# Turning the 64-slot expert's gated rows one step later, in a decoder trunk with a mixture of experts

## The chip, the cores and the metric

The kernel runs on one core of a Trainium2 chip. The metric is device time in microseconds (us) of one execution, lower is better. Five engines matter: TensorE (PE in the profile; its weight loads stand apart as PEld), VectorE (DVE), ScalarE (ACT), GpSimd (POOL) and SyncE (SP), which here only issues the loads of the weights. Each engine runs its own list of instructions in order; they wait for one another through semaphores, which only count up.

## The reference, cut to what matters

Two layers of a decoder run over 256 tokens of width 1024 in fp32. The last feed-forward layer is a mixture of experts: each token goes to 2 of 8 SwiGLU experts with a hidden width of 2816. The change touches only that layer.

```python
def swiglu(x, w1, w2):
    gate, up = jnp.split(x @ w1, 2, axis=-1)
    return (jax.nn.silu(gate) * up) @ w2

def moe_ffn(x, router_w, w1, w2):
    ...
    logits = (xt @ router_w).astype(jnp.float32)
    top_logit, top_idx = lax.top_k(logits, TOP_K)
    gates = jax.nn.softmax(top_logit, axis=-1)
    ...
    def expert_group(args):
        x_blk, e = args
        return swiglu(x_blk, w1[e], w2[e])

    yb = lax.map(expert_group, (xb, blk_expert)).reshape(cap, d)
    yb = yb * slot_gate[:, None].astype(yb.dtype)
    y = jnp.zeros_like(xt).at[slot_tok].add(yb)
```

## The kernel before

**Precision.** A product is made of three or so products of halves: ACT copies a chunk of weights of 128 x 2048 numbers (1 MB) into a rounded high part `whi` (L782, in `split_high`), and DVE subtracts it from the raw chunk, in place, which leaves the low part (L1883, in `split_low`; the trace calls its output `wlo`, `kvXr` or `raw6r` after the buffer). This is called a split here. Some chunks are not split (`WHOLE`): PE multiplies their raw fp32 numbers (L1660).

**Experts in pairs.** The eight experts are ordered by load and taken in four pairs. One of a pair has 128 token slots and is called full ("H"), the other has 64 and is called light ("L"). Each expert has 22 units of work: units 0 to 10 are the first product (two chunks each, giving 256 columns of gate and of up), units 11 to 21 the second product (one chunk each). An H chunk costs PE 12 matmuls (8 if it is not split), an L chunk 8: the light expert's 64 high and 64 low rows fill the 128 rows of the array together.

**Steps.** The function `turns()` gives the steps: step a has unit a % 22 of the full expert of pair a // 22, and the light expert's unit three steps behind (`LAG = 3`). So in steps 11, 12 and 13 of a pair the full expert is in its second product and the light one is still in its first. PE, ACT and DVE each go through the same list of steps with their own part of each, written out by hand. What the text calls step 11 is step 11 of a pair.

**A light unit.** After a light unit j of the first product ACT copies the low rows out of PSUM (L1125), DVE adds them to the high rows (L2478, `lsum`), ACT takes the silu (L1082), DVE multiplies gate by up (L2425, `light_gated`, into half j % 2 of `lgated`, which the trace shows as `arena`), PE transposes the product with two transposes (L1708, in `turn_light`), ACT makes the high copy (L1093, `light_hidden_hi`) and DVE the low copy (L2437, `light_hidden_lo`) in `xhL`. The second product of the light expert reads two rows of `xhL` in each unit (L1689 and L1690). The silu and `light_gated` of unit j stand in the next step, behind the splits which that step's full half asks for.

**Order in a step.** PE: full product; transposes of the full expert's previous unit (L1699); light product; `turn_light`; then, in some steps, spreading, selection or gathering for the next pair (L1585, steps 15 and 18). DVE: splits up to three ahead of the full half's last chunk; `light_gated`; full gating (L2461) and low copy (L2431); splits up to three ahead of the light half's last chunk; `lsum`; `light_hidden_lo`. ACT follows the same plan with its copies.

**Buffers and transfers.** `whi` has three slots (`HRING`): ACT may write the next high part once PE has used the chunk three splits back. Raw chunks have seven slots (`XRING`), and SP issues a load (L610) once PE has used the chunk seven back. A stream of one pair is 66 chunks, of which 58 are split.

Of the kernel before, what the change touches and what calls it, by code (L numbers as in the profile page):

```python
# [34 lines left out]
NF = DFF // P  # L35
# [118 lines left out]
def build(nc, x, mem, par, con, lvl, lin_w, ffn_w, out):  # L154
# [31 lines left out]
    with ExitStack() as ctx:  # L186
# [342 lines left out]
        def pair_no(p, i, j=0):  # L529
            return (p * PAIRS_E + i) * (NF // 2) + j + 1  # L530
# [171 lines left out]
        def _(act):  # L702
# [333 lines left out]
            def experts(p):  # L1036
# [63 lines left out]
                for a, (full, light) in enumerate(turns()):  # L1100
                    if full:
                        i, u = full
                        splits_through(SIDX["H", i, unit_chunks(u)[-1]])
                    if a == 1:
                        first_hi_of("L")
                    if behind:
                        light_silu(*behind)
                        behind = None
                    if full:
                        if u < NF // 2:  # L1110
                            act.wait_ge(w_used, unit_end(p, "H", i, u))
                            nc.scalar.activation(xsilu[:, u % 2, :], pb[:, u % 2, 0:S], ACT.Silu).then_inc(silu_ready, 1)
                        if 1 <= u <= NF // 2:
                            hidden_hi(i, u - 1)
                        if u == UNITS - 1:
                            act.wait_ge(selT_ready, nth(p, i))
                            act.wait_ge(w_used, unit_end(p, "H", i, u))
                            nc.scalar.activation(yHh.rearrange("p (a c) -> p a c", a=2), pb[:, 1:3, :], ACT.Copy,
                                                 scale=gs[:, 0:1]).then_inc(yH_hi, 1)
                    if light:  # L1120
                        i, u = light
                        splits_through(SIDX["L", i, unit_chunks(u)[-1]])
                        if u < NF // 2:
                            act.wait_ge(w_used, unit_end(p, "L", i, u))
                            nc.scalar.activation(low_rows[0:LIGHT, :], pb[LIGHT:P, 3 + u % 2, :], ACT.Copy).then_inc(low_ready, 1)  # L1125
                            behind = light
                        if 1 <= u <= NF // 2:
                            light_hidden_hi(i, u - 1)
                        if u == UNITS - 1 and i < PAIRS_E - 1:
                            act.wait_ge(w_used, unit_end(p, "L", i, u))  # L1130
                            nc.scalar.activation(yLh.rearrange("p (a c) -> p a c", a=2), pb[:, 4:6, :], ACT.Copy,
                                                 scale=gs[:, 1:2]).then_inc(yL_hi, 1)
                    if full:
                        i, u = full
                        if u == 9:
                            selections_turned(i)
                        if u in (15, 18) and i < PAIRS_E - 1:
                            gathered_hi(i + 1, (u - 15) // 3)
# [27 lines left out]
        def _(pe):  # L1166
# [387 lines left out]
            def experts(p):  # L1554
# [164 lines left out]
                for a, (full, light) in enumerate(turns()):  # L1719
                    if full:  # L1720
                        i, u = full
                        if u < NF // 2:
                            first_product("H", i, u)
                        else:
                            second_product("H", i, u - NF // 2).then_inc(w_used, 1)
                        if 1 <= u <= NF // 2:
                            turn_hidden(i, u - 1)
                    if a == 1:
                        gather_first("L")
                    if light and not full and light[1] == UNITS - 2:  # L1730
                        break
                    if light:
                        i, u = light
                        if u < NF // 2:
                            first_product("L", i, u)
                        else:
                            second_product("L", i, u - NF // 2).then_inc(w_used, 1)
                        if 1 <= u <= NF // 2:
                            turn_light(i, u - 1)
                    if full:  # L1740
                        i, u = full
                        if u in (5, 7) and i:
                            spread_outputs(i - 1, (u - 5) // 2)
                        if u == 9:
                            turn_selections(i)
                        if u in (15, 18) and i < PAIRS_E - 1:
                            gather(i + 1, (u - 15) // 3)
# [39 lines left out]
        def _(dve):  # L1787
# [612 lines left out]
            def experts(p):  # L2400
# [20 lines left out]

                def light_gated(i, j):

                    dve.wait_ge(lsilu_ready, pair_no(p, i, j))
                    V.tensor_tensor(lgated[0:LIGHT, j % 2, :], lsilu[0:LIGHT, :], lsum[0:LIGHT, S:2 * S],  # L2425
                                    ALU.mult).then_inc(lg_ready, 1)
# [22 lines left out]
                for a, (full, light) in enumerate(turns()):  # L2449
                    if full:  # L2450
                        i, u = full
                        splits_through(SIDX["H", i, unit_chunks(u)[-1]])
                    if a == 1:
                        first_lo_of(p, "L")
                    if behind:
                        light_gated(*behind)
                        behind = None
                    if full:
                        if u < NF // 2:
                            dve.wait_ge(silu_ready, full_no(p, i, u))  # L2460
                            V.tensor_tensor(xgated[:, u % 2, :], xsilu[:, u % 2, :], pb[:, u % 2, S:2 * S],  # L2461
                                            ALU.mult).then_inc(g_ready, 1)
                        if 1 <= u <= NF // 2:
                            hidden_lo(i, u - 1)
                        if u == UNITS - 1:
                            dve.wait_ge(yH_hi, nth(p, i))
                            V.scalar_tensor_tensor(out=yHl.rearrange("p (a c) -> p a c", a=2), in0=pb[:, 1:3, :],
                                                   scalar=gs[:, 0:1],
                                                   in1=yHh.rearrange("p (a c) -> p a c", a=2).bitcast(F32),
                                                   op0=ALU.mult, op1=ALU.subtract).then_inc(yH_lo, 1)  # L2470
                    if light:
                        i, u = light
                        splits_through(SIDX["L", i, unit_chunks(u)[-1]])
                        if u < NF // 2:
                            if u or i or p:
                                dve.wait_ge(lg_ready, pair_no(p, i, u) - 1)
                            dve.wait_ge(low_ready, pair_no(p, i, u))
                            V.tensor_tensor(lsum[0:LIGHT, :], low_rows[0:LIGHT, :], pb[0:LIGHT, 3 + u % 2, :],  # L2478
                                            ALU.add).then_inc(lsum_ready, 1)
                            behind = light  # L2480
                        if 1 <= u <= NF // 2:
                            light_hidden_lo(i, u - 1)
                        if u == UNITS - 1 and i < PAIRS_E - 1:
                            dve.wait_ge(yL_hi, p * (PAIRS_E - 1) + i + 1)
                            V.scalar_tensor_tensor(out=yLl.rearrange("p (a c) -> p a c", a=2), in0=pb[:, 4:6, :],
                                                   scalar=gs[:, 1:2],
                                                   in1=yLh.rearrange("p (a c) -> p a c", a=2).bitcast(F32),
                                                   op0=ALU.mult, op1=ALU.subtract).then_inc(yL_lo, 1)
                    if full:
                        i, u = full  # L2490
                        if u in (5, 7) and i:
                            add_outputs(i - 1, (u - 5) // 2)
                        if u == 10 and i < PAIRS_E - 1:
                            dve.wait_ge(selT_psum, nth(p, i))
                            select_pair(p, i + 1)
                        if u in (15, 18) and i < PAIRS_E - 1:
                            gathered_lo(i + 1, (u - 15) // 3)
# [113 lines left out]
```

## Time and profile before

| | us |
|---|---|
| median of three runs | 1476.75 (1472.2 to 1478.58) |
| the profiled execution, its own time | 1473.66 |
| its span, first instruction to last | 1471.6 |
| PE busy | 1406.7 (96% of the span) |
| DVE busy | 1100.4 (75%) |
| ACT busy | 904.4 (61%) |

The experts fill the last half of the span, from about 746 us on. A pair takes some 186 us: the wait of step 11 ends at 831.44 in the first pair and at 1018.04 in the second. In this document a time of a row is in us from the start of the span, and an idle time in square brackets is that of the engine just before the row, with what ended it.

### The profile page before, as it was taken

To read this page: it belongs to the slowest core of one execution; us is meant where nothing else is said; L and a number is where in the kernel's file an instruction comes from. 1 tells how busy PE (TensorE), PEld (TensorE's weight loads), DVE (VectorE), ACT (ScalarE), POOL (GpSimd) and SP (SyncE) were. 2 spreads that over 40 slices of the span, in tenths; PEclk is the share of its full clock that TensorE was granted. 3 is DMA by queue.
4 is the path that set the end of the run, shared out by engine and by line. 5 is a ranking of instruction groups with operands and counts; after the bars stand their busy time and mean duration, and the time that the engine had idled before them with its cause. 6 is when DMAs were issued, how large, how long until landed. Compare 5 with 4: busy or idle time off the path is not lost.

```text
span 1471.6 us, 19582 instructions
## 1 busy us (share of the span) xinstructions
PE 1406.7 (96%) x7795; PEld 1163.9 (79%) x7795; DVE 1100.4 (75%) x1188; ACT 904.4 (61%) x997; POOL 52.2 (4%) x58
## 2 busy tenths in 40 slices
PE   8999999999999999999999889998899988999986
PEld 7989898999989989898766676767767667767664
DVE  7878755645546878655778988888888898888986
ACT  6746444444436656444567866777767776777875
POOL 0031000000000031000000000000000000000000
PEclk9999999999999999999999999999999999999999
DMA  8443443445545343545499989999999998999993
GB/s 313 147 143 116 157 158 122 165 173 189 184 173 203 141 144 115 172 146 202 149 369 397 373 334 393 399 358 367 350 393 398 365 375 328 395 391 369 375 357 163
DMA packets 54482, 388.40 MB, mean 264 GB/s; under 512 B 6000, under 2 KB 6256, under 8 KB 8176
## 3 DMA queue, kind: packets, MB, share of 16 engines
q1 hardware_dynamic: 53840, 384.98, 69.1%
q10 hardware_dynamic: 544, 2.10, 0.4%
q8 instruction: 64, 1.05, 0.3%
q14 instruction: 34, 0.28, 0.1%
HBM read 386.00 MB, written 1.05 MB: 263 GB/s over the span
## 4 chain that ended last, share of the span: by engine, by line
issue 52%; PE 45%; DVE 2%; DMA 0%; ACT 0%; POOL 0%; POOLq 0%; DVEq 0%
PE pb L1201 13%; PE pb L1203 12%; PE pb L1202 12%; PE pb L1349 1%; PE pb L1431 1%; PE pb L1451 1%; PE pb L1182 1%; DVE xTl L1853 1%; DMA h<-in_x 0%; PE pb L1441 0%; PE pb L1408 0%; PE pb L1407 0%; PE pb L1300 0%; PE pb L1406 0%; DVE wlo L1804 0%
## 5 line engine op out<-in xcount | busy, mean ns | idle before, releaser
L1883 DVE TENSOR_TENSOR wlo<-raw,whi 128x2048 fp32r<-128x2048 f32 x134 | 303.8, 2285 | 70.3 <-ACT whi L782 69.8
L1804 DVE TENSOR_TENSOR wlo<-raw,whi 128x2048 fp32r<-128x2048 f32 (+1 forms) x101 | 226.0, 2247 | 132.7 <-ACT whi L714 132.3
L782 ACT ACTIVATE whi<-raw 128x2048 fp32r<-128x2048 f32 x134 | 254.6, 1914 | 101.1 <-PE pb L1203 63.8
L714 ACT ACTIVATE whi<-raw 128x2048 fp32r<-128x2048 f32 (+1 forms) x101 | 190.1, 1884 | 172.9 <-PE pb L1203 164.3
L1201 PE MATMUL pb<-xTh,whi 128*128 128x256 f32 x736 | 210.0, 285 | 2.0 <-DVE xTl L1841 1.2
L1202 PE MATMUL pb<-xTl,whi 128*128 128x256 f32 x736 | 208.2, 283 | 0.0
L1203 PE MATMUL pb<-xTh,wlo 128*128 128x256 f32 x736 | 208.2, 283 | 0.0
L1883 DVE TENSOR_TENSOR kvXr<-kvX,whi 128x2048 fp32r<-128x2048 f32 x65 | 147.8, 2285 | 29.8 <-ACT whi L782 29.5
L782 ACT ACTIVATE whi<-kvX 128x2048 fp32r<-128x2048 f32 x65 | 123.9, 1913 | 47.1 <-PE pb L1203 25.7
L1201 PEld LDWEIGHTS pb<-xTh,whi 128*128 128x128 f32 x736 | 141.1, 192 | 3.5 <-issue 1.9
L1657 PE MATMUL pb<-whi,xg 128*128 128x512 f32 x352 | 141.2, 401 | 1.1 <-DVE wlo L1883 0.7
L1202 PEld LDWEIGHTS pb<-xTl,whi 128*128 128x128 f32 x736 | 141.2, 192 | 0.1
L1203 PEld LDWEIGHTS pb<-xTh,wlo 128*128 128x128 f32 x736 | 141.1, 192 | 0.0
L1201 PE MATMUL pb<-whi,xg 128*128 128x512 f32 x224 | 90.8, 406 | 1.0 <-DVE wlo L1883 0.6
L1203 PE MATMUL pb<-whi,xg 128*128 128x512 f32 x224 | 88.0, 393 | 0.0
L1201 PE MATMUL pb<-whi,xTh 128*128 128x512 f32 (+1 forms) x224 | 86.1, 385 | 0.7 <-DVE xTl L1853 0.6
L1203 PE MATMUL pb<-whi,xTl 128*128 128x512 f32 (+1 forms) x224 | 84.4, 377 | 0.0
L1202 PE MATMUL pb<-wlo,xTh 128*128 128x512 f32 (+1 forms) x224 | 84.3, 376 | 0.0
L1883 DVE TENSOR_TENSOR raw6r<-arena,whi 128x2048 fp32r<-128x2048 f32 x33 | 75.3, 2283 | 10.6 <-ACT whi L782 10.3
L1657 PEld LDWEIGHTS pb<-whi,xg 128*128 128x128 f32 x352 | 66.2, 188 | 16.4 <-issue 2.3
L1658 PE MATMUL pb<-wlo,xg 128*128 128x512 f32 x200 | 78.3, 391 | 0.0
L1201 PE MATMUL pb<-whi,xhTh 128*128 128x512 f32 x176 | 75.2, 428 | 1.1
(410 smaller groups left out, 2823.1 us busy)
## 6 DMA issues: line engine op xcount, KB each, us to landing
raw<-in_ffn_w SPq DMA_DIRECT2D x184, 1024.0 KB, 7.1
kvX<-in_ffn_w SPq DMA_DIRECT2D x76, 1024.0 KB, 7.3
raw<-in_lin_w SPq DMA_DIRECT2D x64, 1024.0 KB, 4.9
arena<-in_ffn_w SPq DMA_DIRECT2D x37, 1024.0 KB, 7.3
raw<-in_lin_w SPq DMA_DIRECT2D x4, 536.0 KB, 5.4
arena<-in_mem ACTq DMA_DIRECT2D x2, 1024.0 KB, 7.9
h<-in_x SPq DMA_DIRECT2D x1, 1024.0 KB, 5.1
out<-xn SPq DMA_DIRECT2D x2, 512.0 KB, 3.1
```

The lines of the kernel that those rows point to most:

```text
L714: nc.scalar.activation(whi[:, m % HRING, c], raw[:, m % RING, c], ACT.Copy).then_inc(hi_ready, 1)
L782: nc.scalar.activation(whi[:, split_no(p, n) % HRING, :], xraw_slots[slot], ACT.Copy).then_inc(hi_ready, 1)
L1182: mm = nc.tensor.transpose(pb[:, turn_bank(no, b), i * S + t * P:i * S + (t + 1) * P], xn[:, t, k * P:(k + 1) * P], ident)
L1201: nc.tensor.matmul(o, lh, rh, start=first, stop=False)
L1202: nc.tensor.matmul(o, lh, rl, start=False, stop=False)
L1203: return nc.tensor.matmul(o, ll, rh, start=False, stop=last)
L1349: mm = nc.tensor.matmul(pb[:, b + hd % 2, i * P:(i + 1) * P], K[r, o + t * P:o + (t + 1) * P], Q[r, o + t * P:o + (t + 1) * P], start=True ...
L1431: mm = nc.tensor.matmul(pb[:, 4 + hd, t * S:(t + 1) * S], qX[:, 2 * hd + k, t * P:(t + 1) * P], kX[:, 2 * hd + k, :], start=(k == 0), stop ...
L1657: nc.tensor.matmul(o, both, w[0][:, kk, :], start=first, stop=False)
L1658: mm = nc.tensor.matmul(o, both, w[1][:, kk, :], start=False, stop=last)
L1804: V.tensor_tensor(wlo[:, m % RING, c], raw[:, m % RING, c], whi[:, m % HRING, c].bitcast(F32), ALU.subtract).then_inc(lo_ready, 1)
L1883: V.tensor_tensor(xlo_slots[slot], xraw_slots[slot], whi[:, split_no(p, n) % HRING, :].bitcast(F32), ALU.subtract).then_inc(lo_ready, 1)
```

## The change

`turn_light`, `light_hidden_hi` and `light_hidden_lo` of unit j run in the step of light unit j + 2 instead of j + 1, on PE, ACT and DVE alike. Since the transposes of unit j - 2 may now still be to come when `light_gated` wants to write unit j into the same half of `lgated`, DVE gets a wait for them.

```diff
@@ ACT
-                        if 1 <= u <= NF // 2:
-                            light_hidden_hi(i, u - 1)
+                        if 2 <= u <= NF // 2 + 1:
+                            light_hidden_hi(i, u - 2)
@@ PE
-                        if 1 <= u <= NF // 2:
-                            turn_light(i, u - 1)
+                        if 2 <= u <= NF // 2 + 1:
+                            turn_light(i, u - 2)
@@ DVE
                 def light_gated(i, j):
 
+                    if p or i or j >= 2:
+                        dve.wait_ge(lhid_turned, pair_no(p, i, j) - 2)
                     dve.wait_ge(lsilu_ready, pair_no(p, i, j))
...
-                        if 1 <= u <= NF // 2:
-                            light_hidden_lo(i, u - 1)
+                        if 2 <= u <= NF // 2 + 1:
+                            light_hidden_lo(i, u - 2)
```

In the middle of a pair the engines' lists read the same as before, since each step still has one pair of transposes; they belong to the unit before. The lists differ at the two ends. PE, the first step that had transposes of the light expert (step 4, `-`) and the first that has them now and had none (step 15, `+`, ahead of the gathering for the next pair):

```order
@@ -4128,5 +4128,4 @@
 L1657 MATMUL pb<-whi,xg 128x512
 L1658 MATMUL pb<-raw6r,xg 128x512
-L1708 MATMUL pb<-consts,arena 128x64 x2
 L1201 MATMUL pb<-whi,xg 128x512
 L1202 MATMUL pb<-kvXr,xg 128x512
@@ -4468,4 +4467,5 @@
 L1689 MATMUL pb<-whi,xhL 128x512
 L1690 MATMUL pb<-kvXr,xhL 128x512
+L1708 MATMUL pb<-consts,arena 128x64 x2
 L1585 MATMUL pb<-sel,xnh 128x192
 L1585 MATMUL pb<-sel,xnl 128x192
```

The last pair of transposes of a light expert moved from the end of step 14, where the light product of unit 11 ends, to the end of step 15. ACT, the same two places; its high copy in step 15 stands between the splits and the copies of the gathered rows (L1068):

```order
@@ -425,5 +425,4 @@
 L782 ACTIVATE whi<-raw 128x2048 [waits w_used,x_loaded3]
 L1125 ACTIVATE arena<-pb 64x512 [waits w_used]
-L1093 ACTIVATE xhL<-pb 128x2x64 [waits lhid_turned]
 L782 ACTIVATE whi<-raw 128x2048 [waits w_used,x_loaded4]
 L1082 ACTIVATE arena<-arena 64x256 [waits lsum_ready]
@@ -503,4 +502,5 @@
 L782 ACTIVATE whi<-raw 128x2048 [waits w_used,x_loaded3]
 L782 ACTIVATE whi<-raw 128x2048 [waits w_used,x_loaded4]
+L1093 ACTIVATE xhL<-pb 128x2x64 [waits lhid_turned]
 L1068 ACTIVATE xg<-pb,params 128x192 [waits gathered]
 L1068 ACTIVATE xg<-pb,params 128x192
```

One high copy left the list at step 4 and one came in at step 15. DVE in the middle of a pair, before:

```order
L1883 TENSOR_TENSOR kvXr<-kvX,whi 128x2048 [waits hi_ready]
L2425 TENSOR_TENSOR arena<-arena 64x256 [waits lsilu_ready]
L2461 TENSOR_TENSOR xgated<-xsilu,pb 128x256 [waits silu_ready]
L2431 TENSOR_TENSOR xhTl<-pb,xhTh 128x256 [waits hT_hi]
L1883 TENSOR_TENSOR wlo<-raw,whi 128x2048 [waits hi_ready] x2
```

and DVE at the same place in the changed kernel, whose lines from L2424 on are numbered two higher:

```order
L1883 TENSOR_TENSOR kvXr<-kvX,whi 128x2048 [waits hi_ready]
L2427 TENSOR_TENSOR arena<-arena 64x256 [waits lsilu_ready,lhid_turned]
L2463 TENSOR_TENSOR xgated<-xsilu,pb 128x256 [waits silu_ready]
L2433 TENSOR_TENSOR xhTl<-pb,xhTh 128x256 [waits hT_hi]
L1883 TENSOR_TENSOR wlo<-raw,whi 128x2048 [waits hi_ready] x2
```

The gated product kept its place behind the splits and has one wait more. SP's list is the same in both.

## Rows read from the trace of the kernel before

**Rows 1.** Waits, 760 to 1471 us: who waited <- for whom: total, times, longest.

```profile
PE pb L1708 <- DVE arena L2425: 34.2, 24, 2.9
...
PE pb L1657 <- DVE wlo L1883: 0.7, 2, 0.4
```

**Rows 2.** Windows: PE, PEld, DVE, ACT, POOL busy (count), granted clock, DMA share, GB/s.

```profile
748.00:1453.00 705.00, 666.49 (x2755) 490.20 (x2753) 603.40 (x515) 516.18 (x487) 0.00 (x0) 0.99 0.95 370
...
817.40:857.70 40.30, 32.39 (x139) 24.88 (x138) 39.46 (x36) 32.12 (x31) 0.00 (x0) 0.96 0.98 375
```

**Rows 3.** Timeline, PE, first pair, steps 7 and 10 to 16: start, duration, instruction, idle.

```profile
789.05 0.34 PE L1708 MATMUL pb<-consts,arena 64*128 64x64 f32 x2 [0.83 <-DVE arena L2425]
...
822.25 0.34 PE L1708 MATMUL pb<-consts,arena 64*128 64x64 f32 x2 [0.83 <-DVE arena L2425]
822.52 0.50 PE L1201 MATMUL pb<-whi,xhTh 128*128 128x512 f32 x1
...
831.44 0.34 PE L1708 MATMUL pb<-consts,arena 64*128 64x64 f32 x2 [1.99 <-DVE arena L2425]
...
839.51 0.33 PE L1708 MATMUL pb<-consts,arena 64*128 64x64 f32 x2 [1.10 <-DVE arena L2425]
...
847.52 0.33 PE L1708 MATMUL pb<-consts,arena 64*128 64x64 f32 x2 [1.10 <-DVE arena L2425]
...
855.53 0.47 PE L1708 MATMUL pb<-consts,arena 64*128 64x64 f32 x2 [2.89 <-DVE arena L2425]
855.94 0.79 PE L1201 MATMUL pb<-whi,xhTh 128*128 128x512 f32 x1
...
861.22 0.54 PE L1689 MATMUL pb<-whi,xhL 128*128 128x512 f32 x1
...
863.20 0.25 PE L1585 MATMUL pb<-sel,xnh 128*128 128x192 f32 x1
...
864.97 0.41 PE L1201 MATMUL pb<-whi,xhTh 128*128 128x512 f32 x1
...
867.72 0.39 PE L1689 MATMUL pb<-whi,xhL 128*128 128x512 f32 x1
```

**Rows 4.** Timeline, DVE, first pair, steps 10 to 15.

```profile
819.58 2.29 DVE L1883 TENSOR_TENSOR wlo<-raw,whi 128x2048 fp32r<-128x2048 f32 x1 [0.46 <-ACT whi L782]
...
828.77 2.28 DVE L1883 TENSOR_TENSOR raw6r<-arena,whi 128x2048 fp32r<-128x2048 f32 x1
...
836.84 2.27 DVE L1883 TENSOR_TENSOR wlo<-raw,whi 128x2048 fp32r<-128x2048 f32 x1
839.04 0.41 DVE L2425 TENSOR_TENSOR arena<-arena 64x256 f32<-64x256 f32 x1
...
844.85 2.29 DVE L1883 TENSOR_TENSOR wlo<-raw,whi 128x2048 fp32r<-128x2048 f32 x1 [0.19 <-ACT whi L782]
...
852.86 2.29 DVE L1883 TENSOR_TENSOR kvXr<-kvX,whi 128x2048 fp32r<-128x2048 f32 x1 [0.19 <-ACT whi L782]
...
863.47 4.49 DVE L1883 TENSOR_TENSOR wlo<-raw,whi 128x2048 fp32r<-128x2048 f32 x2 [5.59 <-ACT whi L782]
```

**Rows 5.** Windows around the stretches at half clock, columns as in Rows 2.

```profile
854.00:862.00 8.00, 6.47 (x17) 5.10 (x18) 3.88 (x4) 1.68 (x3) 0.00 (x0) 0.57 0.60 254
1018.00:1023.00 5.00, 4.96 (x16) 3.94 (x17) 5.00 (x4) 1.66 (x3) 0.00 (x0) 0.66 0.91 383
1226.00:1234.00 8.00, 6.38 (x17) 5.02 (x18) 3.97 (x4) 1.68 (x3) 0.00 (x0) 0.57 0.63 253
1414.00:1419.00 5.00, 5.00 (x16) 3.95 (x16) 1.93 (x2) 0.68 (x2) 0.00 (x0) 0.66 0.63 264
```

**Rows 6.** Windows of 20 us, DMA in the last two columns.

```profile
850.00:870.00 20.00, 17.11 (x73) 13.82 (x72) 14.06 (x18) 11.39 (x12) 0.00 (x0) 0.83 0.76 297
...
890.00:910.00 20.00, 19.88 (x75) 13.41 (x74) 15.47 (x9) 12.47 (x9) 0.00 (x0) 1.00 1.01 421
```

**Rows 7.** Timeline, PE, the wait of step 14 in the second pair.

```profile
1043.65 0.27 PE L1708 MATMUL pb<-consts,arena 64*128 64x64 f32 x1 [2.91 <-DVE arena L2425]
```

## The prediction

> **What bounds the kernel now.** I read the waits first, then the windows, then the timelines of PE and DVE side by side. The waits say that PE, in the whole stretch of the experts, waits for one thing: 34.2 us in 24 places before L1708, the transposes of the light expert, for DVE's gated product L2425; the next cause, a split, is 0.7 us [rows 1]. The window over the experts has PE busy 666.5 of 705 us [rows 2], so most of its idle time is this wait. The timeline shows where: in each pair six times, in step 7 (0.83 us) and in steps 10 to 14 (0.83, 1.99, 1.10, 1.10, 2.89; 7.91 us together) [rows 3]. The other three pairs repeat it.
>
> Why is the gated product late? DVE runs it behind the splits of its step: the split from 836.84 to 839.11, then L2425 at 839.04, then PE goes on at 839.51 [rows 3, 4]. And DVE is full there: busy 39.5 of 40.3 us in 817.4 to 857.7 [rows 2]. So from step 10 to 14 DVE, not PE, sets the pace, and the decisive question is not how much PE waits at L1708 but for what it would wait in its place: the low part of the chunk of its next product, which the same DVE makes just ahead of the gated product.
>
> The last wait is of another kind. At 852.64 PE has done step 14's products, and the splits of step 15 are done or due soon, but it stands until 855.53 for a product whose transposes nobody needs soon. Because PE uses nothing meanwhile, whi's three slots stay full, ACT can't copy, and DVE then idles 5.59 us before 863.47 [rows 4]. PE also runs at half its clock after it: granted clock 0.57 over 854 to 862 and over 1226 to 1234, and 0.66 over 1018 to 1023 and 1414 to 1419 [rows 5], which is 6.9, 6.9, 3.4 and 3.4 us at the level of 1.2 GHz.
>
> **The change part by part.** *The wait at L1708.* With the transposes of unit j - 2 instead of j - 1, the gated product that they need was made a whole step earlier, 7 to 10 us before. The 34.2 us go as waits of L1708. I follow the first pair to see what takes their place. Work of PE in a step is the distance of two L1708 rows less the idle time of the second: 7.20, 6.97, 6.91 and 5.12 us for steps 11 to 14, of which the transposes are 0.27 (822.25 to 822.52) [rows 3].
> - Step 10 ends for PE at 821.42. Transposes, 821.69. The split of step 11's first chunk ends at 821.87 [rows 4]; PE starts at 821.9 (before 822.52).
> - Step 11: 6.93 more, 828.8, transposes 829.1; but the next chunk's split ends at 831.05 [rows 4]. DVE has no gap before it, so nothing that PE does earlier brings it forward. Start 831.1 (before 831.7).
> - Step 12: 6.70, 837.8, transposes 838.1; split ends 839.11. Start 839.15 (before 839.8).
> - Step 13: 6.64, 845.8, 846.1; split ends 847.14, of which DVE's gap of 0.19 goes, since ACT gets its slot earlier. Start 847.0 (before 847.8).
> - Step 14: 4.85, 851.85, transposes 852.1, with no wait. Step 15: the full product takes 2.75 (864.97 to 867.72), 854.9; the light chunk's split, 855.15 before, is 0.4 earlier without the two gaps of 0.19, so just in time; 1.9 for the light product (861.22 to 863.20 was 1.98, a little of it at half clock); transposes 0.27; gathering 1.77 (863.20 to 864.97): step 16 starts at 858.8.
>
> Before, step 16 started at 864.97 [rows 3]. So the pair gains 6.15 us: of 7.91 us of waits some 4.5 us stay, as waits for splits, 3.45 go, and 2.7 are the clock: the full product of step 15 took 5.28 (855.94 to 861.22) instead of 2.75, the transposes 0.41 instead of 0.27. In step 7, PE would go on at 788.22 + 0.27, and only the split just ahead of the gated product holds it, 0.33 us before L2425 ends; there 0.6 of 0.83 goes. For the waits alone: 4 x (3.45 + 0.6) = 16.2 us.
>
> *The clock.* The half-clock stretches cost 2.7 us where PE came out of the long wait into one of 6.9 us (twice), and 1.7 us, half of 3.4, where all of it was work (twice): 8.8 us [rows 3, 5]. Three of the four are next to a wait of 2.9 us, the one at 1018 to a wait of 1.96; but the wait of 2.91 at 1043.65 [rows 7] has none. The longest wait that I expect to stay is some 2 us (829.1 to 831.1). So the two long stretches should go, and I count one of the short ones as staying: 8.8 - 1.7 = 7.1 us.
>
> *DVE's new wait* (44 times). Behind it queue the splits. It asks for transposes of unit j - 2, which PE issues right after light product j, while the same L2425 already needs that product, ACT's copy, `lsum` and the silu. It is met when DVE comes there. The row with two waits, if it cost anything, would leave gaps, and DVE has 0.8 us of idle time in 40 us [rows 2]. I take nothing; from the other side, that idle time spent again in each pair would be 3 us.
>
> *The copies one step later on ACT and DVE.* The same number of instructions. In step 15 one copy comes in on each; DVE has 5.59 us of idle time after it [rows 4]. Who needs the result? The second product reads unit c's rows in step c + 14, the copies of unit 0 now come in step 5, those of unit 10 in step 15 for step 24. Nothing. The transfers: SP's list is unchanged, its loads start when PE lets a slot go, so earlier.
>
> *What is late next.* After step 15 DVE and PE both run 6 us earlier, and DVE's gap of 5.59 us is gone. The transfers had pauses there (share 0.76, 297 GB/s) [rows 6]. A pair moves 66 chunks, 69.2 MB; in 186.6 - 6.75 = 180 us that is 385 GB/s against 371 now. The window 890 to 910 shows 421 GB/s at a share of 1.01 [rows 6], so they should keep up, with less in hand.
> The Trainium skill speaks against it: "DMA: Bandwidth & Descriptors", Specifications, gives about 358 GB/s as what HBM yields to one core. By that rule a pair could not be under 69.2 / 0.358 = 193 us, the transfers would already be the bound and the change would bring nothing. The trace disagrees: 370 GB/s over 705 us, 421 in a window.
>
> **Sum.** 16.2 + 7.1 = 23.3 us off the profiled execution's own 1473.66: 1450.4. The three runs lie 1.5 us below to 4.9 above that execution, their median 3.1 above; the median less the same sum is 1453.5. I take 1452, about midway, which is to count from 1475.3; the rivals below count from there too.
>
> **The rivals.**
> - *The clock stays.* Waits of some 2, 1 and 1 us for splits remain in steps 11 to 13, and the fall at 1018 came after such a one. Then only the 16.2 us go: 1459.
> - *DVE takes back nearly all.* Each wait turns into one for the split that ends 0.33 us before the gated product's end, and the lead of PE after step 14 is lost again between steps 16 and 21, where DVE has two splits of 2.29 for each 4.6 us of PE's work. Then 24 x 0.4, about 10 us: 1465. Against it: DVE idles 5.59 us there now, so it gains the lead together with PE.
> - *The transfers take over.* If a pair can't be faster than at some 380 GB/s, 182 us, the four gain 4 to 4.5 each: 1458. If the loads were at their bound already, nothing: 1475. (The page's rule above would be such a case.)
> - *All of it goes*, 34.2 and 8.8 us: 1432. It would need DVE to have slack in steps 10 to 14; the rows say no.
> - *Slower.* PE's few long waits become more and shorter ones. If the granted clock fell after each of those instead of once in a pair, at 3 us a time for work at 1.2 GHz, it has to eat the 16 us of the waits and the 8.8 us of today: eight falls of 3 us break even, and twelve (steps 11 to 13 of all four pairs) would give 1475.3 - 16.2 - 8.8 + 36 = 1486. Against it: at 831.44 a wait of 1.99 brings no fall now.
> - *It doesn't do what it says.* The order on all three engines shows that it does; nothing left of this.
>
> **How the numbers follow.** Forecast 0.60, clock stays 0.14, DVE takes back 0.08, transfers 0.09 (0.02 of it for loads at their bound already), all goes 0.05, slower 0.04. The range goes from 1442, short of the case in which all goes, to 1467, which takes in the clock, the transfers at 380 GB/s, DVE's 10 us and the 3 us of the new wait. Half a per cent, 7.4 us, is about what a measurement of this kernel can tell from no change. Faster by more: 0.88. Within: 0.08, from loads at their bound and the tails of the second and third rival. Slower by more: 0.04.
>
> **What would show it.** No wait of L1708 for L2425. In its place waits of L1201 for `wlo` and its like, three in each pair near 2, 1 and 0.9 us, 14 to 18 us in all, and none at the end of step 14. DVE's gap of 5.59 us gone, and at most two half-clock stretches in the experts. The distance from pair to pair 179 to 181 us. If the waits of ACT on transfers grow beyond PE's reach, or PE waits for splits in steps 16 to 21, the second or third rival holds. The weakest step is the clock, whose falls I can't tie to one length of wait.

## The result and the profile after

The changed kernel takes 1453.37 us in the median of four runs (1449.95 to 1454.34), against 1477.65 for the kernel before in the runs beside it. The ratio is 0.984, with a 95% interval of 0.981 to 0.987: 24 us faster. The prediction said 1452, in a range of 1442 to 1467. The ratios in this document leave out one execution of 6308.7 us, of the kernel with both edits, the only one out of line.

The profiled execution has a span of 1447.9 us, 23.7 less than before. First the waits, as in [rows 1] (who waited <- for whom: total, times, longest):

```profile
PE pb L1201 <- DVE wlo L1883: 7.9, 11, 1.5
...
PE pb L1708 <- DVE xhL L2439: 2.9, 4, 0.8
PE pb L1201 <- DVE kvXr L1883: 2.8, 4, 0.7
PEld pb L1657 <- DVE wlo L1883: 2.7, 8, 0.5
...
PEld pb L1657 <- DVE kvXr L1883: 2.2, 6, 0.5
...
PE pb L1201 <- DVE raw6r L1883: 1.8, 2, 1.5
```

The 34.2 us before L1708 for the gated product are gone. In their place PE waits for splits (L1883), under each of the names that a low part has, and, four times, before L1708 for something that the prediction didn't name: the low copy L2439. The window over the experts (columns as in [rows 2]) shows DVE as busy in us as before and PE 4.7 us less, in 23 us less, at a granted clock of 1.00; the transfers moved 383 GB/s instead of 370:

```profile
748.00:1430.00 682.00, 661.78 (x2758) 483.56 (x2757) 603.43 (x516) 516.52 (x487) 0.00 (x0) 1.00 0.97 383
```

The timeline of PE in the first pair, which answers to [rows 3], has the first row of the full product of steps 11 to 14, the transposes at the end of step 14, the start of step 15, the transposes at its end, and the start of step 16:

```profile
821.49 0.47 PE L1201 MATMUL pb<-whi,xhTh 128*128 128x512 f32 x1 [0.34 <-DVE wlo L1883]
830.66 0.47 PE L1201 MATMUL pb<-whi,xhTh 128*128 128x512 f32 x1 [1.50 <-DVE raw6r L1883]
838.73 0.47 PE L1201 MATMUL pb<-whi,xhTh 128*128 128x512 f32 x1 [0.71 <-DVE wlo L1883]
846.47 0.47 PE L1201 MATMUL pb<-whi,xhTh 128*128 128x512 f32 x1 [0.71 <-DVE wlo L1883]
...
852.01 0.31 PE L1708 MATMUL pb<-consts,arena 64*128 64x64 f32 x2 [0.70 <-DVE xhL L2439]
852.25 0.50 PE L1201 MATMUL pb<-whi,xhTh 128*128 128x512 f32 x1
...
856.98 0.33 PE L1708 MATMUL pb<-consts,arena 64*128 64x64 f32 x2
...
859.11 0.42 PE L1201 MATMUL pb<-whi,xhTh 128*128 128x512 f32 x1
```

Five waits of 3.96 us together stand where 7.91 us stood. Step 16 starts at 859.1 instead of 864.97. DVE's idle 5.59 us [rows 4] have shrunk to 0.48:

```profile
851.00 0.67 DVE L2480 TENSOR_TENSOR arena<-arena,pb 64x512 f32<-64x512 f32 x1
851.59 0.27 DVE L2439 TENSOR_TENSOR xhL<-pb,xhL 128x128 fp32r<-128x128 f32 x1
...
857.29 2.29 DVE L1883 TENSOR_TENSOR wlo<-raw,whi 128x2048 fp32r<-128x2048 f32 x1 [0.48 <-ACT whi L782]
```

The row at 851.59 is the low copy of unit 8: it ends at 851.86, and the transposes of unit 9, which write the same PSUM bank, start at 852.01. In the trace of before the low copy at the same place of DVE's list is this one:

```profile
852.39 0.28 DVE L2437 TENSOR_TENSOR xhL<-pb,xhL 128x128 fp32r<-128x128 f32 x1
```

It ended at 852.67, just when PE came there (852.64), and the wait for the gated product hid it. Now PE comes at 851.31.

### The profile page after: what moved, and what is told of

Same layout as the page of the kernel before. It is cut to its first block, busy times and chain, and to the rows that moved or that the text cites. A ratio compares the mean times of both kernels' runs of the same rounds, so it can differ in the third digit from the quotient of the medians.

```text
span 1447.9 us, 19624 instructions
## 1 busy us (share of the span) xinstructions
PE 1401.6 (97%) x7795; PEld 1156.8 (80%) x7795; DVE 1098.8 (76%) x1188; ACT 904.1 (62%) x997; POOL 52.2 (4%) x58
## 4 chain that ended last, share of the span: by engine, by line
issue 51%; PE 46%; DVE 2%; DMA 0%; ACT 0%; POOL 0%; POOLq 0%; DVEq 0%
PE pb L1201 13%; PE pb L1203 13%; PE pb L1202 13%; PE pb L1349 1%; PE pb L1431 1%; PE pb L1451 1%; PE pb L1182 1%; DVE xTl L1853 1%; DMA h<-in_x 0%; PE pb L1441 0%; PE pb L1408 0%; PE pb L1407 0%; PE pb L1300 0%; PE pb L1406 0%; DVE wlo L1804 0%
## 5 line engine op out<-in xcount | busy, mean ns | idle before, releaser
L1883 DVE TENSOR_TENSOR wlo<-raw,whi 128x2048 fp32r<-128x2048 f32 x134 | 303.6, 2283 | 51.1 <-ACT whi L782 50.8
L1883 DVE TENSOR_TENSOR kvXr<-kvX,whi 128x2048 fp32r<-128x2048 f32 x65 | 147.7, 2283 | 29.8 <-ACT whi L782 29.6
L1201 PE MATMUL pb<-whi,xhTh 128*128 128x512 f32 x176 | 71.6, 407 | 13.2 <-DVE wlo L1883 7.6
L1883 DVE TENSOR_TENSOR raw6r<-arena,whi 128x2048 fp32r<-128x2048 f32 x33 | 75.3, 2283 | 6.9 <-ACT whi L782 6.7
```

The lines of the kernel that those rows point to most:

```text
L1201: nc.tensor.matmul(o, lh, rh, start=first, stop=False)
L1883: V.tensor_tensor(xlo_slots[slot], xraw_slots[slot], whi[:, split_no(p, n) % HRING, :].bitcast(F32), ALU.subtract).then_inc(lo_ready, 1)
```

## The experiments

A measure that is free of what happens ahead of the experts is useful for the comparisons: the distance from the end of step 12 in the first pair to the same point in the fourth, divided by three. It is the time of a pair; it takes in what happens in steps 13 and 14 of three of the four pairs. For the kernel before it is (1397.56 - 839.51) / 3 = 186.0 us, for the changed one (1377.10 - 837.69) / 3 = 179.8, from these rows of before and of after:

```profile
1397.56 0.34 PE L1708 MATMUL pb<-consts,arena 64*128 64x64 f32 x2 [1.15 <-DVE arena L2425]
```

```profile
837.69 0.34 PE L1708 MATMUL pb<-consts,arena 64*128 64x64 f32 x2
...
1377.10 0.33 PE L1708 MATMUL pb<-consts,arena 64*128 64x64 f32 x2
```

| kernel | ratio to before (95%) | a pair, us |
|---|---|---|
| before | 1 | 186.0 |
| changed | 0.984 (0.981 to 0.987) | 179.8 |
| changed, measured again | 0.982 (0.979 to 0.986) | 179.8 |
| before + DVE's wait alone | 0.999 (0.996 to 1.001) | 186.0 |
| before, last unit alone moved | 0.989 (0.986 to 0.993) | 180.9 |
| before + matmuls in the waits, 18 in step 14 | 0.999 (0.996 to 1.001) | 185.0 |
| before + matmuls in the waits, 12 in step 14 | 0.994 (0.992 to 0.995) | 183.9 |
| before, silu and gated product ahead of the splits | 1.008 (1.006 to 1.011) | 189.1 |
| changed, low copy ahead of the sum | 0.984 (0.981 to 0.988) | 179.7 |
| changed, one chunk more unsplit | 0.982 (0.979 to 0.985) | 179.3 |
| changed, both | 0.983 (0.979 to 0.986) | 179.2 |
| before, six raw slots | 1.005 (1.002 to 1.007) | 187.9 |
| changed, six raw slots | 0.987 (0.984 to 0.990) | 181.4 |

The changed kernel measured again had a median of 1448.55 us, where I had expected 1450 to 1455; its ratio and its pair agree with the first measurement.

**The last unit alone.** Only unit 10's transposes and copies go to step 15; the same two lines are changed for `light_hidden_hi` and `light_hidden_lo`, and DVE has its new wait.

```diff
-                        if 1 <= u <= NF // 2:
-                            turn_light(i, u - 1)
+                        if 1 <= u <= NF // 2 - 1 or u == NF // 2 + 1:
+                            turn_light(i, min(u - 1, NF // 2 - 1))
```

> The kernel before with DVE's new wait, and only the transposes and copies of the last light unit (10) moved, from step 14 to step 15; units 0 to 9 stay where they were. My theory: the wait of 2.89 us at the end of step 14 is the one that costs, since it alone stops PE while nothing of its next work is missing, and the clock's fall hangs on it. PE would go on at 852.65 instead of 855.94: 4 x 3.3 = 13 us, and 7 to 9 us of the clock, so 20 to 22 us faster than before, 1455 to 1457, hardly behind the full change. The waits of steps 10 to 13 stay as waits of L1708 (0.8, 2.0, 1.1, 1.1). Rival, each wait of the 34.2 us is worth its length: 11.6 us of them go and the clock partly, 12 to 15 us in all.

The waits of steps 10 to 13 stayed as they were, the one of step 14 went, and nothing took its place:

```profile
PE pb L1708 <- DVE arena L2427: 22.5, 20, 2.0
```

Two rows of its timeline, the end of step 13 and the start of step 15's full product:

```profile
852.50 0.27 PE L1708 MATMUL pb<-consts,arena 64*128 64x64 f32 x1 [1.10 <-DVE arena L2427]
...
857.48 0.39 PE L1201 MATMUL pb<-whi,xhTh 128*128 128x512 f32 x1
```

These are 4.98 us apart, where before 847.52 to 855.94 was 8.42: 3.4 us for a wait of 2.89 and the transposes behind it. No half-clock stretch is left in the experts (granted clock 1.00 over 748 to 1440), although a wait of some 2.0 us stays at the end of step 11 of each of the first three pairs. The pair takes 180.9 us: one of the eleven units brings 5.1 of the 6.2 us. In the time it is 15.8 us (0.989), less than the 20 expected; the last section tells of what lies between the executions. The rival, that each of the waits is worth its length, would have given 12 to 15 us with the clock, which the time alone doesn't exclude (its interval is 10 to 21 us); the pair's time does, with 5.1 us in each of the four pairs: 2.1 for the clock, by the 12 matmuls below, and 3.0 for the wait of 2.89.

**DVE's wait alone.** The two lines in `light_gated`, nothing else.

> The kernel before with DVE's new wait for the transposes of unit j - 2, always met there, and nothing else. My theory: it costs nothing, ratio 1.00 within the interval, no new idle time of DVE. Rival: each wait takes a fraction of a tenth of a us of DVE where DVE is full (16 places), up to 1 us and not to be seen in the time; or DVE's idle time in steps 10 to 14 doubles, 3 us.

Ratio 0.999, the same 186.0 us a pair, the same wait of PE to 0.1 us in 34:

```profile
PE pb L1708 <- DVE arena L2427: 34.1, 24, 2.9
```

The wait costs nothing that can be seen.

**The clock by itself.** Matmuls of the identity that nobody reads fill PE's idle time, and leave what it waits for where it was: 8 in step 11, for the waits of 1.99 us, and 18 in step 14, for those of 2.89.

```diff
+                        if u in (8, NF // 2):
+                            for _ in range(8 if u == 8 else 18):
+                                nc.tensor.matmul(pb[:, 0, 0:P], ident, ident, start=True, stop=True)
                         if 1 <= u <= NF // 2:
                             turn_light(i, u - 1)
```

> The kernel before with idle-time matmuls on PE whose results nobody reads (8 at the end of step 11's light product, 18 at the end of step 14's, 128 x 128 fp32 into a bank that is free there), ahead of the waiting transposes. They shorten no wait's end; the four half-clock stretches are what they can remove. My theory: these cost 8.8 us, and some 6 to 9 us go, 1467 to 1470 against 1476; PE's idle time at the end of step 14 shrinks from 2.9 to about 1 us while the transposes start at the same distance from step 13's. Rival: the clock's fall costs nothing of its own, since PE waits for splits anyway, and the time stays.

The clock stayed at full speed through the experts, but the time moved by 0.1% only. The fill was too long. This row of its timeline has the 18 matmuls (each stands as two in the trace, so x36), which end 1.1 us later than the wait of before ended (at 855.53):

```profile
852.44 4.18 PE L1740 MATMUL pb<-consts 128*128 128x128 f32 x36
...
856.55 0.33 PE L1708 MATMUL pb<-consts,arena 64*128 64x64 f32 x2
```

My guess of their length was wrong: they take 0.232 us each, and to leave about 1 of 2.9 us idle, as I had expected, they would have to take 0.1. So once more, with 12:

> As the kernel with idle-time matmuls before, but 12 instead of 18 at the end of step 14: the 18 took 4.18 us (0.232 each) where the wait was 2.89, and put the transposes 1.1 us later in each pair, 4.4 us in all. 12 take 2.8 us. My theory: the trace's stretch of the experts, which was 3.5 us shorter than before's with 18, is now some 8 us shorter, the price of the half-clock stretches: 1465 to 1468. Rival: the clock costs 3.5 us, and the stretch doesn't shorten further.

```profile
850.29 2.84 PE L1740 MATMUL pb<-consts 128*128 128x128 f32 x24
...
853.34 0.33 PE L1708 MATMUL pb<-consts,arena 64*128 64x64 f32 x2 [0.20 <-DVE arena L2428]
```

Now the transposes start 8.0 us after those of step 13, as before, and the window over the place that had a granted clock of 0.57 [rows 5] has 1.00:

```profile
853.00:862.00 9.00, 8.80 (x49) 7.45 (x48) 6.00 (x5) 5.25 (x7) 0.00 (x0) 1.00 0.93 356
```

Every wait for DVE is as long as it was, counting the fill, and the kernel is 0.6% faster, 9.3 us. In the trace a pair is 2.1 us shorter, some 8 us over the experts, and that is the price of the half-clock stretches alone; my estimate was 8.8. The rest of the 9.3 can't be told from what differs between executions ahead of the experts. Which of the two fills removed which stretch was not tried apart.

The trace of before has a second measure of the same price, since not every pair of it has a half-clock stretch. The end of step 12 in its second and third pair:

```profile
1027.63 0.27 PE L1708 MATMUL pb<-consts,arena 64*128 64x64 f32 x1 [1.09 <-DVE arena L2425]
...
1211.59 0.27 PE L1708 MATMUL pb<-consts,arena 64*128 64x64 f32 x1 [1.12 <-DVE arena L2425]
```

From 839.51 to 1027.63, with the stretches at 854 and 1018, it takes 188.1 us; from there to 1211.59, with none, 184.0; and from there to 1397.56, with the one at 1226, 186.0. The distance without a stretch is that of the kernel with 12 matmuls, 183.9.

**The same wait removed from the other side.** On ACT the silu, and on DVE the gated product, go to the head of the next step, ahead of the splits of the full half.

```diff
+                    if behind:
+                        light_gated(*behind)
+                        behind = None
                     if full:
                         i, u = full
                         splits_through(SIDX["H", i, unit_chunks(u)[-1]])
...
-                    if behind:
-                        light_gated(*behind)
-                        behind = None
```

> The kernel before with the light expert's silu (ACT) and gated product (DVE) at the head of the next step, ahead of the splits that the full half asks for; the transposes stay one step behind. It removes the same wait from the other side. My theory: the transposes were late because the gated product stands behind a split. The waits of L1708 go (below 4 us in all), PE then waits for splits in steps 10 to 13, and DVE pays by standing about 0.5 us for ACT's silu in each of the 44 units, 16 of them where DVE is full: some 8 us of the 23 are given back, 1457 to 1463. Rival, the place behind the splits is not the cause: the 34 us of waits stay.

This was slower than before, by 0.8%. The waits of L1708 did nearly go, but in the list of waits another stands on top:

```profile
ACT arena L1082 <- DVE arena L2478: 108.3, 43, 3.0
...
PE pb L1201 <- DVE wlo L1883: 15.4, 7, 2.9
```

ACT, in the first pair:

```profile
839.42 0.42 ACT L1082 ACTIVATE arena<-arena 64x256 f32<-64x256 f32 x1 [2.89 <-DVE arena L2478]
839.75 5.50 ACT L782 ACTIVATE whi<-raw 128x2048 fp32r<-128x2048 f32 x3
```

ACT stands 2.89 us for the sum, which DVE has behind the splits of the light half. The high copies behind it come late, so do the splits, and PE waits up to 2.9 us for them in steps 11 and 13. The clock has a part in it too, since the trace has eight half-clock stretches in the experts where before has four. One of them stands in a window in which before has 1.00:

```profile
1041.00:1049.00 8.00, 6.69 (x23) 5.10 (x23) 6.78 (x6) 5.12 (x6) 0.00 (x0) 0.79 0.81 308
```

How the 0.8% divides between the waits and the clock was not tried. I had priced DVE's wait for the silu (it measures 10.2 us in all, in 34 places) and overlooked ACT's for the sum. The place of the gated product was the cause of the wait, but not a place that can be moved alone.

**The wait that the prediction had missed.** In the changed kernel DVE's low copy goes ahead of the sum.

```diff
+                        if 2 <= u <= NF // 2 + 1:
+                            light_hidden_lo(i, u - 2)
                         if u < NF // 2:
                             ...
                             V.tensor_tensor(lsum[0:LIGHT, :], low_rows[0:LIGHT, :], pb[0:LIGHT, 3 + u % 2, :],
                                             ALU.add).then_inc(lsum_ready, 1)
                             behind = light
-                        if 2 <= u <= NF // 2 + 1:
-                            light_hidden_lo(i, u - 2)
```

> The changed kernel with one line moved on DVE: the light low copy (which frees the PSUM bank that the next transposes write) stands ahead of the sum of the light rows instead of behind it. It tests the wait that the prediction had not seen: 0.70 to 0.76 us in step 14 of each pair, where the transposes of unit 9 wait for the low copy of unit 8. My theory: that copy is late only because DVE is behind, and the sum of 0.6 us stands ahead of it, so 0.6 of 0.7 us goes in each pair, 2 to 2.5 us in all, a ratio of 0.998 to the changed kernel, to be seen in the trace rather than in the time. Rival: the wait turns into one for step 15's split and nothing is won.

The wait left step 14, as the theory has it, but most of it came back in step 15, where the transposes of unit 10 now wait for the low copy of unit 9:

```profile
855.82 0.30 PE L1708 MATMUL pb<-consts,arena 64*128 64x64 f32 x2
...
861.36 0.30 PE L1708 MATMUL pb<-consts,arena 64*128 64x64 f32 x2 [0.49 <-DVE xhL L2439]
```

A pair is 0.1 us shorter, not 0.6. The theory was right on the place and wrong on the gain.

**A split less where DVE is full.** Unit 10's second chunk is left unsplit, in the changed kernel.

```diff
-WHOLE = (0, 1, 2, 4, 5, 6, 8, 9)
+WHOLE = (0, 1, 2, 4, 5, 6, 8, 9, 10)
```

> The changed kernel with unit 10's second chunk of the full expert not split (multiplied raw, as in units 8 and 9). It takes one split (2.29 us of DVE, 1.9 of ACT) out of step 10, where DVE's full stretch begins, and gives PE 8 fp32 matmuls for 12, some 0.8 us more. My theory: PE's waits for splits in steps 10 to 13 (3.3 us in a pair) and that of 0.7 in step 14 stay only because DVE is full from step 10 on; with a split less they go nearly all, 4.0 - 0.8 = some 3 us in a pair, 9 to 12 us in all, 1441 to 1444, ratio to before 0.976 to 0.978. Rival, DVE's chain of steps 10 to 14 hangs on the three high slots rather than on its own work: the waits stay and the kernel is 3 us slower than the changed one.

A pair takes 179.3 us instead of 179.8, a sixth of what I expected. The waits of steps 12 and 13 stand at 0.71 as in the changed kernel, that of step 14 at 0.69, and that of step 11 went from 1.50 to 1.27. A row of DVE and one of ACT in step 10 tell why:

```profile
819.83 4.50 DVE L1883 TENSOR_TENSOR wlo<-raw,whi 128x2048 fp32r<-128x2048 f32 x2 [2.20 <-ACT whi L782]
```

```profile
817.88 3.74 ACT L782 ACTIVATE whi<-raw 128x2048 fp32r<-128x2048 f32 x2 [1.45 <-PE pb L1658]
```

DVE is no longer full there, it idles 2.20 us, because ACT waits for a high slot that PE hasn't let go. What DVE does not do it can't do ahead: the three high slots bound its lead, as the rival said, though the kernel isn't the 3 us slower that it asked for. That is read from the waits; no kernel with a fourth slot was run. From step 11 on the pace is DVE's own again. So my reading that the waits of steps 10 to 13 come from DVE's load alone was incomplete; they need both. With both edits the time was 0.983 of before, a pair 179.2:

> Both edits on the changed kernel. My theory: with a split less DVE is no longer behind in step 14, so the low copy's place brings nothing on top of the unsplit chunk: the same time as that kernel alone, 1441 to 1444. Rival: the two add, 1439 to 1441.

The two edits add up to 0.1 us in a pair over the unsplit chunk alone; the intervals of all four kernels overlap. Both kernels miss the expected 1441 to 1444 us, with medians of 1447.6 and 1451.5. By the traces the two kernels with the unsplit chunk are the best, by half a microsecond in a pair. No measured time here tells them from the changed kernel.

**The transfers.** Six slots for raw chunks instead of seven (`XRING = 6`), on the kernel before and on the changed one.

> The kernel before with six slots for raw chunks instead of seven, so that each load starts a chunk later. It measures the slack of the transfers. Landing to the end of the split is 4.3 us where ACT stands waiting for the load, and the longest stretch without a DVE gap there leaves PE 3 to 5 us in hand; a chunk is 2.7 us. My theory: the slack is about one slot, so it costs 0 to 10 us before.

> The changed kernel with six slots. The rival of the prediction on transfers said that the faster kernel stands closer to them. My theory: it does, since a pair is 6 us shorter at the same 66 chunks and the pause of the transfers after step 14 is gone: the change is worth less with six slots than with seven (24 us), by 3 to 10 us. Rival, transfers are not near: the change is worth 24 us here too.

The one costs 0.5%; the other costs 0.3 to 0.5%, by which of the two measurements of the changed kernel it is held against. The medians are 1482.0 and 1456.0, so that the change is worth 26 us there too. My theory, that it is worth less, fell. ACT does wait for loads then; the first row is the changed kernel's, the second that of before, both with six slots:

```profile
ACT whi L782 <- DMA raw<-in_ffn_w: 90.8, 65, 3.7
```

```profile
ACT whi L782 <- DMA raw<-in_ffn_w: 82.4, 54, 3.7
```

but a pair of the changed kernel grows by only 1.6 us, and one of the kernel before by 1.9. With seven slots ACT's waits for loads are 31.8 us before and after alike (17.5, 12.9 and 1.4 for the three kinds of slot after). By these rows the transfers were not what the faster kernel ran into.

## Why the prediction held, and where it did not

**What bounds it.** The reading that DVE sets the pace in steps 10 to 14, so that the waits there shrink instead of going, was right, though incomplete: the kernel with a split less shows that the three high slots hold DVE back too. The starts of the full product were foreseen at 821.9, 831.1, 839.15, 847.0 and 858.8 for steps 11 to 14 and 16. The execution after is 0.6 us ahead when it comes there (step 10's light product ends at 820.82 instead of 821.42); with that added its rows give 822.1, 831.3, 839.3, 847.1 and 859.7.

**The wait of step 14.** The prediction held that PE goes on with no wait there. It waits 0.70 to 0.76 us in each pair, 2.9 in all. I had asked for the gated product of each unit, and not for the other thing that `turn_light` waits for, that the PSUM bank has been emptied of the unit before. Before, that copy ended at 852.67 and the gated product only at 855.48, so the first wait hid the second; the working had PE there at 851.85, and the row at 852.39 would have shown that the copy isn't done then. This is the working's error of mechanism in step 14, and most of step 16's 0.9 us.

**Waits that stay.** Foreseen near 2, 1 and 0.9 us in steps 11 to 13, 14 to 18 in all; measured 1.50, 0.71 and 0.71 in the first pair and 12.5 in all (7.9 + 2.8 + 1.8), those of steps 10 and 7 with them. So fewer than foreseen are waits of PE; the rest is hidden, since PE's weight loads (PEld) now wait 2.7 + 2.2 us for splits inside the light products of steps 11 to 13, against 0.3 + 0.2 before. In step 7 the prediction let 0.6 of 0.83 us go; in the first pair 0.33 are left, in the others there is no wait at all.

**The clock.** I counted 8.8 us and one short stretch as staying, 7.1. None stayed in the experts, in this execution and in a second one of the same kernel, and the fill of 12 matmuls prices the stretches at about 8 us. So the price was 0.8 us too high and the 1.7 for a stretch that stays too much; they cancel in part.

**The sum.** 23.3 foreseen, 23.7 measured in the spans. By a pair's time: 6.2 us, of which 2.1 are the clock (the fill), 3.0 the last unit's move, and 1.1 the moves of the other ten units.

That the sum came so near is partly luck. Lay the starts of the same product of PE in both traces side by side (847.78 and 846.47 for step 14, 855.94 and 852.25 for step 15, and so on); the difference grows by these amounts, in us over the four pairs:

| where | foreseen | measured |
|---|---|---|
| step 4, which has no transposes any more | not counted | 1.7 |
| step 7 | 2.4 | 3.2 |
| steps 10 to 13 | 3.2 | 3.1 |
| step 14 | 12.2 | 9.2 |
| the half-clock stretches | 7.1 | 8.2 |
| step 15, which has transposes now | -1.1 | -1.3 |

Steps 10 to 13, where the working is longest, are right. The 3.0 us that the overlooked wait took from step 14 were given back by three items that were too low, above all the transposes of step 4, whose going the prediction didn't count although it charged step 15 for them. (The column of the measured adds up to 24.1, of which 0.5 are lost again ahead of the experts; that of the foreseen to 23.8 for rounding in the working.)

**Rivals.** "The clock stays" fell with the granted clock of 1.00. "DVE takes back nearly all" fell because DVE's idle 5.59 us went too. "The transfers take over" asked for pairs of 182 us; they take 179.8, and six slots cost the changed kernel no more than the one before. The limit of some 358 GB/s that the Trainium skill gives ("DMA: Bandwidth & Descriptors", Specifications) stands against 383 over 682 us, so the trace doesn't bear it out for this kernel. The slower rival didn't show; the kernel with the silu moved forward shows that such a one was near at hand: its loss begins with a wait of ACT, which I had not named, but it also has the more numerous falls of the clock that I had.

## What to carry to other kernels

When a wait stands behind an engine that is full, ask what that engine makes next for the same waiter: most of the wait only changes its name. The one that is worth its whole length, and more, is the wait in which the waiter's next work is already there, since it also stops the buffers behind it and, here, let the clock fall. List every semaphore that the moved instruction waits for, not only the one in the profile: the second comes out once the first is gone. And an instruction moved forward on one engine waits there in front of all that is queued behind it.

## What the runs showed of the hardware

Idle-time matmuls kept the granted clock at 1.00 through waits of 2.9 us after which it had been 0.57, and were worth 0.6% by themselves, some 8 us over the experts. The length of a single wait doesn't decide on the fall: 1.96 us at 1018 had one, 2.91 at 1043.65 had none [rows 5, 7]. Nor does its place in the kernel: the kernel with DVE's wait alone, whose waits are those of before to 0.1 us, has one behind the wait that ends step 11 of the first pair,

```profile
833.31 0.33 PE L1708 MATMUL pb<-consts,arena 64*128 64x64 f32 x2 [1.97 <-DVE arena L2427]
```

```profile
833.00:838.00 5.00, 4.69 (x14) 3.69 (x15) 5.00 (x5) 1.93 (x3) 0.00 (x0) 0.66 0.94 392
```

where before, with a wait of 1.99 at 831.44, has none. What does decide stays open.

Executions of the changed kernel lie 4 to 5 us apart, and its two profiles show one place for it, ahead of the experts. The window of 700 to 722 us, where the router's short operations leave PE idle, in the changed kernel's profile and in that of its second measurement:

```profile
700.00:722.00 22.00, 20.43 (x114) 16.16 (x113) 19.17 (x73) 13.49 (x24) 0.00 (x0) 0.92 0.23 82
```

```profile
700.00:722.00 22.00, 19.49 (x94) 15.89 (x95) 17.00 (x61) 11.25 (x19) 0.00 (x0) 0.77 0.08 26
```

The granted clock is 0.92 in the one and 0.77 in the other, and the spans are 1447.9 and 1452.0 us, with pairs of the same 179.8 us. The kernel with only the last unit moved was profiled in an execution of the second kind too (span 1456.5). It is not the only place: the kernel with DVE's wait alone has 0.92 there like the one before, and its span is 3.4 us longer, most of it by the stretch at 833 and by a granted clock of 0.87 instead of 0.93 over 722 to 748. What puts the other timed runs apart was not tried.
